# Up-projection of split activations with one 512-column matmul per k-tile, its two bank halves added on evacuation

## The reference

```python
def conv_geglu_ffn(x, w_up, conv_w, conv_b, w_down):      # once; D_FF = 5504
    up = einsum('bsd,df->bsf', x, w_up)                   # 2048 -> 2 * 5504
    u = pad(up, 2 rows in front)
    u = sum(u[:, j:j + S] * conv_w[j] for j in range(3)) + conv_b
    gate, val = split(u, 2, axis=-1)
    y = gelu(gate, approximate=True) * val
    return einsum('bsf,fd->bsd', y, w_down)

def second_ffn(x, w1, w2):                                # twice; 2048 -> 8192 -> 2048
    return square(relu(x @ w1)) @ w2
```

## Time and profile before

| what | value |
|---|---|
| median of 3 runs | 3329.59 us (3329.06 to 3329.69) |
| span of the profiled execution, first to last instruction | 3327.3 us |
| mean granted TensorE clock | 0.986 |
| first up stage, 86 units | about 467 to 964 us |
| second up stage, 64 units | about 1540 to 1910 us |
| third up stage, 64 units | about 2593 to 2963 us |

### The profile page before, as it was taken

The page is one execution under the profiler, slowest core; times in us unless marked ns, Lnnn a source line. Parts: engine busy times, 40 slices in busy tenths (PEclk is TensorE's granted clock), DMA queues, the critical chain, the costliest instruction groups (busy, mean ns, idle before and its releaser), DMA issues.

```text
span 3327.3 us, 54721 instructions
## 1 busy us (share of the span) xinstructions
PE 3210.2 (96%) x21428; PEld 2969.3 (89%) x21428; DVE 1948.1 (59%) x2303; ACT 1510.5 (45%) x1684; POOL 11.0 (0%) x25
## 2 busy tenths in 40 slices
PE   7999989999999979998999999998999899999998
PEld 7999779999998879878999988888988899998886
DVE  6666566566554469866444444448985644444445
ACT  5565554444444444654333444444654433344443
POOL 0000000000000000000000000000000000000000
PEclk9999999999999989999999999999999999999999
DMA  6444435554555544344455555554435455555553
GB/s 223 153 158 157 175 145 186 177 188 176 185 220 197 192 141 159 146 146 157 178 188 177 183 220 189 194 197 150 143 125 194 152 178 187 177 215 189 192 197 127
DMA packets 81366, 585.27 MB, mean 176 GB/s; under 512 B 9072, under 2 KB 9072, under 8 KB 11392
## 3 DMA queue, kind: packets, MB, share of 16 engines
q1 hardware_dynamic: 78912, 567.78, 47.6%
q0 software_dynamic: 2368, 16.35, 1.3%
HBM read 581.99 MB, written 2.10 MB: 176 GB/s over the span
## 4 chain that ended last, share of the span: by engine, by line
PE 90%; DVE 4%; issue 2%; ACT 2%; DMA 1%; DVEq 0%; SPq 0%; ACTq 0%
PE bank L536 35%; PE bank L524 17%; PE bank L526 17%; PE bank L525 17%; DVE store L1485 1%; DVE w_lo L1192 1%; ACT w_hi L847 1%; PE bank L567 1%; DMA raw<-units 1%; PE bank L573 0%; PE bank L693 0%; PE bank L692 0%; PE bank L691 0%; ACT L962 0%; PE bank L723 0%
## 5 line engine op out<-in xcount | busy, mean ns | idle before, releaser
L1192 DVE TENSOR_TENSOR w_lo<-raw,w_hi 128x2048 fp32r<-128x2048 f32 x543 | 1230.9, 2268 | 870.7 <-ACT y_hi L851 575.3
L524 PE MATMUL bank<-x_hi,w_hi 128*128 128x256 f32 x4928 | 1402.7, 285 | 8.1 <-DVE x_lo L1213 5.6
L525 PE MATMUL bank<-x_lo,w_hi 128*128 128x256 f32 x4928 | 1395.7, 283 | 0.0
L526 PE MATMUL bank<-x_hi,w_lo 128*128 128x256 f32 x4928 | 1395.7, 283 | 0.0
L847 ACT ACTIVATE w_hi<-raw 128x2048 fp32r<-128x2048 f32 x543 | 1028.6, 1895 | 703.5 <-PE bank L536 644.4
L524 PEld LDWEIGHTS bank<-x_hi,w_hi 128*128 128x128 f32 x4928 | 947.0, 192 | 12.3 <-DVE w_lo L1192 6.9
L525 PEld LDWEIGHTS bank<-x_lo,w_hi 128*128 128x128 f32 x4928 | 947.3, 192 | 0.2
L526 PEld LDWEIGHTS bank<-x_hi,w_lo 128*128 128x128 f32 x4928 | 947.0, 192 | 0.0
L536 PE MATMUL bank<-w_hi,y_hi 128*128 128x512 f32 x1752 | 470.2, 390 | 11.3 <-DVE y_lo L1195 6.1
L536 PE MATMUL bank<-w_lo,y_hi 128*128 128x512 f32 x1752 | 469.9, 390 | 0.0
L536 PE MATMUL bank<-w_hi,y_lo 128*128 128x512 f32 x1752 | 469.9, 390 | 0.0
(11 more groups left out here) (209 smaller groups left out, 1398.5 us busy)
## 6 DMA issues: line engine op xcount, KB each, us to landing
raw<-units SPq DMA_DIRECT2D x527, 1024.0 KB, 4.8
gain_b<-rows POOLq DMA_DIRECT2D x7, 1024.0 KB, 7.4
bias_b<-rows POOLq DMA_DIRECT2D x6, 1024.0 KB, 9.7
raw<-units SPq DMA_DIRECT2D x8, 768.0 KB, 4.2
raw<-units SPq DMA_DIRECT2D x8, 512.0 KB, 3.7
x<-x_in SPq DMA_DIRECT2D x2, 1024.0 KB, 8.4
out<-x SPq DMA_DIRECT2D x2, 1024.0 KB, 3.9
store<-attn_consts POOLq DMA_DIRECT2D x1, 1024.0 KB, 14.8
```

The lines of the kernel that those rows point to most:

```text
L524: pe.matmul(acc, hi, x_hi[:, k, :], start=(k == 0), stop=False)
L525: pe.matmul(acc, hi, x_lo[:, k, :], start=False, stop=False)
L526: mm = pe.matmul(acc, lo, x_hi[:, k, :], start=False, stop=(k == KT - 1))
L1192: ins = dve.tensor_tensor(w_lo[:, slot, 0:width], raw[:, slot, 0:width], w_hi[:, slot, 0:width].bitcast(F32), ALU.subtract)
```

## The change

In the up stages `x_hi` and `x_lo` lie side by side for each k-tile in one tensor `x_hl`. For each k-tile one matmul of 512 columns moves both past w_hi: x_hi goes to the first half of the bank, x_lo to the second. A second matmul of 256 columns adds w_lo with x_hi to the first half. From the second k-tile on the narrow matmul is issued ahead of the wide one. The two halves of the bank have to be added: ScalarE copies the second half out (`up_low_half`), VectorE adds the first half to it (`up_sum`), and the bank is free after that (`up_added`). In the first block the middle tap, its scale and bias move to VectorE as a tensor_scalar on `up_sum`, and the other taps read `up_sum` in place of the bank. In the second block ReLU and square become one instruction on VectorE. The two new tiles lie in the space of `lat_lo`. The other stages read `x_hi` and `x_lo` as views of the new tensor.

```diff
-        x_hi = sb("x_hi", [P, KT, S], F32R)
-        x_lo = sb("x_lo", [P, KT, S], F32R)
+        x_hl = sb("x_hl", [P, KT, 2, S], F32R)
+        x_hi, x_lo = x_hl[:, :, 0, :], x_hl[:, :, 1, :]
...
+        up_low_half, up_sum = (sb(n, [P, S], offset=at[0] - 4 * S * (QT + VT - i)) for i, n in enumerate(
+            ("up_low_half", "up_sum")))
...
+            def wide_unit(stage, turn, s, layer, acc, x_event=None):
+
+                pe.wait_ge(lo_done, unit_of(stage, turn, s, layer) + 1)
+                slot = stage.slot(s)
+
+                def high(k):
+                    return pe.matmul(acc[:, :], w_hi[:, slot, k * P:(k + 1) * P], x_hl[:, k, :, :],
+                                     start=(k == 0), stop=(k == KT - 1))
+
+                def low(k):
+                    return pe.matmul(acc[:, 0:S], w_lo[:, slot, k * P:(k + 1) * P], x_hi[:, k, :],
+                                     start=False, stop=False)
+
+                for k in range(KT):
+                    if x_event is not None and k % 2 == 0:
+                        pe.wait_ge(xt_lo, x_event * 8 + (k // 2 + 1))
+                    if k == 0:
+                        high(k)
+                    low(k)
+                    if k:
+                        mm = high(k)
+                mm.then_inc(unit_mm, 1)
...
             def up1(turn, s):
                 if not first_turn(turn):
-                    pe.wait_ge(conv_done, turn * 3 + (s - 2))
-                column_unit(UP1, turn, s, 0, bank[s][:, 0:S], x_event=1 if first_turn(turn) and s == 0 else None)
+                    pe.wait_ge(up_added, turn * 3 + (s - 2))
+                wide_unit(UP1, turn, s, 0, bank[s], x_event=1 if first_turn(turn) and s == 0 else None)
...
-                    act.activation(x_hi[:, 2 * b:2 * b + 2, :].rearrange("p a c -> p (a c)"), bank[b][:, :],
+                    act.activation(x_hi[:, 2 * b:2 * b + 2, :], bank[b][:, :].rearrange("p (a c) -> p a c", a=2),
                                    ACT.Copy).then_inc(xt_hi, 1)
...
-                    act.activation((ffn_gate, ffn_val)[n][:], bank[s][:, 0:S], ACT.Identity,
-                                   scale=column(cols1, first + 2, pair * 8), bias=column(cols1, first + 3, pair * 8)
-                                   ).then_inc(conv_base, 1)
+                    if not (first_turn(turn) and s == 0):
+                        act.wait_ge(up_added, pair * 2 + n)
+                    act.activation(up_low_half[:], bank[s][:, S:2 * S], ACT.Copy).then_inc(up_low, 1)
...
-                    act.activation(ffn_gate[:], bank[s][:, 0:S], ACT.Relu).then_inc(relu_read, 1)
+                    act.wait_ge(up_added, layer * FT2 + 2 * FT1 + i)
+                    act.activation(up_low_half[:], bank[s][:, S:2 * S], ACT.Copy).then_inc(up_low, 1)
...
-                    dve.wait_ge(conv_base, pair * 2 + (n + 1))
-                    chain = Chain(dve, conv_step, pair * 2 + n, 1)
-                    chain.link(dve.scalar_tensor_tensor(to[:, 1:S], acc[:, 0:S - 1], column(cols1, first + 1, pair * 8),
+                    dve.wait_ge(up_low, pair * 2 + (n + 1))
+                    chain = Chain(dve, conv_step, pair * 2 + n, 2)
+                    if not (first_turn(pair) and n == 0):
+                        dve.wait_ge(conv_done, pair * 2 + n)
+                    dve.tensor_tensor(up_sum[:], bank[s][:, 0:S], up_low_half[:], ALU.add).then_inc(up_added, 1)
+                    dve.wait_ge(up_added, pair * 2 + (n + 1))
+                    chain.link(dve.tensor_scalar(to[:], up_sum[:], column(cols1, first + 2, pair * 8),
+                                                 column(cols1, first + 3, pair * 8), ALU.mult, ALU.add))
+                    chain.link(dve.scalar_tensor_tensor(to[:, 1:S], up_sum[:, 0:S - 1], column(cols1, first + 1, pair * 8),
                                                         to[:, 1:S], ALU.mult, ALU.add))
-                    dve.scalar_tensor_tensor(to[:, 2:S], acc[:, 0:S - 2], column(cols1, first, pair * 8),
+                    dve.scalar_tensor_tensor(to[:, 2:S], up_sum[:, 0:S - 2], column(cols1, first, pair * 8),
                                              to[:, 2:S], ALU.mult, ALU.add).then_inc(conv_done, 1)
...
-                    dve.wait_ge(relu_read, layer * FT2 + i + 1)
-                    dve.tensor_tensor(slot_at(i), ffn_gate[:], ffn_gate[:], ALU.mult).then_inc(y2_ready, 1)
+                    dve.wait_ge(up_low, layer * FT2 + 2 * FT1 + i + 1)
+                    if not (first_turn(turn) and s == 0):
+                        dve.wait_ge(y2_ready, layer * FT2 + i)
+                    dve.tensor_tensor(up_sum[:], bank[s][:, 0:S], up_low_half[:], ALU.add).then_inc(up_added, 1)
+                    dve.wait_ge(up_added, layer * FT2 + 2 * FT1 + i + 1)
+                    dve.scalar_tensor_tensor(slot_at(i), up_sum[:], 0.0, up_sum[:], ALU.max, ALU.mult).then_inc(y2_ready, 1)
```

More of the change, by code:

```diff
@@ L379, in build @@
             "qd_step", "kd_step", "d_maxstep", "d_normstep", "d_rsstep", "d_mixstep"))
-        conv_base, conv_done, conv_step, gelu_done, y_ready = (sem(n) for n in (
-            "conv_base", "conv_done", "conv_step", "gelu_done", "y_ready"))
+        up_low, up_added = sem("up_low"), sem("up_added")
+        conv_done, conv_step, gelu_done, y_ready = (sem(n) for n in ("conv_done", "conv_step", "gelu_done", "y_ready"))
         (pad_zero, gate_ready, h_ready, dw_step, c_copied, c_ms, c_rs, c_rsstep, c_step, cn_ready, c_hi, c_lo,
@@ L402, in build @@
         diag_ready, last_conv, last_copied = sem("diag_ready"), sem("last_conv"), sem("last_copied")
-        relu_read, y2_ready = sem("relu_read"), sem("y2_ready")
+        y2_ready = sem("y2_ready")
         stored = sem("stored")
@@ L674, in _ @@
                 row_begin(DOWN1, s, 0, 1)
-            pe.wait_ge(conv_done, 2 * FT1)
+            pe.wait_ge(up_added, 2 * FT1)
             row_stage(DOWN1, 0, 1)
@@ L821, in up2 @@
                     if not first_turn(turn):
-                        pe.wait_ge(relu_read, layer * FT2 + turn * 3 + (s - 2))
-                    column_unit(UP2, turn, s, layer, bank[s][:, 0:S],
-                                x_event=layer * 2 + 3 if first_turn(turn) and s == 0 else None)
+                        pe.wait_ge(up_added, layer * FT2 + (2 * FT1 - 2) + turn * 3 + s)
+                    wide_unit(UP2, turn, s, layer, bank[s],
+                              x_event=layer * 2 + 3 if first_turn(turn) and s == 0 else None)
                 for s in range(SLOTS):
@@ L830, in _ @@
                     row_begin(DOWN2, s, layer, 1)
-                pe.wait_ge(relu_read, (layer + 1) * FT2)
+                pe.wait_ge(up_added, (layer + 1) * FT2 + 2 * FT1)
                 row_stage(DOWN2, layer, 1)
@@ L1020, in up1_pair @@
                     act.wait_ge(unit_mm, unit_of(UP1, turn, s, 0) + 1)
[L1021 to L1026, removed]
-                    act.activation((ffn_gate, ffn_val)[n][:], bank[s][:, 0:S], ACT.Identity,
-                                   scale=column(cols1, first + 2, pair * 8), bias=column(cols1, first + 3, pair * 8)
-                                   ).then_inc(conv_base, 1)
+                    if not (first_turn(turn) and s == 0):
+                        act.wait_ge(up_added, pair * 2 + n)
+                    act.activation(up_low_half[:], bank[s][:, S:2 * S], ACT.Copy).then_inc(up_low, 1)
                 act.wait_ge(conv_done, pair * 2 + 1)
+                if not first_turn(pair):
+                    act.wait_ge(y_ready, pair)
                 act.activation(ffn_act[:], ffn_gate[:], ACT.Gelu_apprx_tanh).then_inc(gelu_done, 1)
@@ L1170, in up2 @@
                     act.wait_ge(unit_mm, unit_of(UP2, turn, s, layer) + 1)
-                    if not (first_turn(turn) and s == 0):
-                        act.wait_ge(y2_ready, layer * FT2 + i)
-                    act.activation(ffn_gate[:], bank[s][:, 0:S], ACT.Relu).then_inc(relu_read, 1)
+                    act.wait_ge(up_added, layer * FT2 + 2 * FT1 + i)
+                    act.activation(up_low_half[:], bank[s][:, S:2 * S], ACT.Copy).then_inc(up_low, 1)
                 for s in range(SLOTS):
@@ L1212, in transposed @@
                     at_ = (slice(None), slice(2 * b, 2 * b + 2), slice(None))
-                    dve.tensor_tensor(x_lo[at_].rearrange("p a c -> p (a c)"), bank[b][:, :],
-                                      x_hi[at_].rearrange("p a c -> p (a c)").bitcast(F32), ALU.subtract).then_inc(xt_lo, 1)
+                    dve.tensor_tensor(x_lo[at_], bank[b][:, :].rearrange("p (a c) -> p a c", a=2),
+                                      x_hi[at_].bitcast(F32), ALU.subtract).then_inc(xt_lo, 1)
             def sharpened(eps, chain, *roots):
@@ L1406, in up1_pair @@
                     first = COLS1["conv"][0] + 4 * n
-                    acc, to = bank[s], (ffn_gate, ffn_val)[n]
-                    dve.wait_ge(conv_base, pair * 2 + (n + 1))
-                    chain = Chain(dve, conv_step, pair * 2 + n, 1)
```

(6 more changed lines are left out.)

## The result

The changed kernel takes 3305.36 us (median of 4 runs, 3303.59 to 3306.39), the kernel before 3329.64 us (3329.06 to 3329.93). The ratio is 0.9928, with a 95% interval of 0.9916 to 0.9940. The gain is 24.3 us where 45.0 us were forecast, and the time lies 7 us above the upper end of the range.

The account below looks back on a forecast made before the run. TensorE was taken as the bound, busy 96% of the span. Saving 45.7 us over 214 units, less 0.6 us for first units, all else free, gave -45.0 us: 3329.6 to 3284.6 us, range 3279 to 3298.

Parts of the forecast that it names:

- Point 1: TensorE, up stages' steady state: a k-tile falls from 360.0 to 346.7 ns, 213 ns a unit, 45.7 us over 214 units.
- The surplus goes by matmul, not by column: TensorE steps: each matmul, of 256 or 512 columns, carries 13.3 ns beyond its column time, saved with each matmul removed.
- The prediction's own last sign of being wrong: Profile after, up stages: the forecast is wrong if the wide matmul's step is longer than 0.227 us.
- VectorE did not bind: Rival, 6%: VectorE becomes the bound in the first up stage; 18.3 us of gain lost, 3302.9 us.
- The surplus did not belong to w_hi and w_lo: Rival, 4%: the surplus comes from changing between w_hi and w_lo, the removed step nearly free; time stays 3329.6 us.
- A narrow step was at times 6.7 ns shorter: Rival, 4%: a narrow matmul behind a wide one has no surplus; k-tile 333.3 ns, gain 90 us, 3239.6 us.
- No load stood in the open: Rival, 2%: the wide matmul's load can't run beside the narrow one before it; 327 us slower, 3657 us.
- Point 2: First unit of each of three up stages gains nothing, since unit 1 waits for w_lo; 0.6 us taken off.
- Points 3, 4, 6: ScalarE's copies, second-block VectorE work (3.2 us plus links in 5.55 us), banks freed about 1 us after: all cost nothing.
- Point 7: Transfers, SP and POOL: none added; 1 MB a unit in 5.55 us, 189 GB/s, under the down stage's 197 GB/s.
- Point 5: VectorE, first block, the tight place: a pair takes 10.0 us of TensorE's 11.09 us, fitting with 1.1 us to spare.
- Point 8: Interleaved x_hi and x_lo, transposes' evacuations writing two runs of 256: taken as nothing, bound 2.9 us.

Follow-up runs that it names:

- e9: Changed kernel with each unit's narrow matmuls in one group, each moving 128 columns instead of 256, same load of 128 weights: 3270.83 us.
- e11: Changed kernel with each unit's narrow matmuls in one group, each moving 128 columns and loading 64 weight columns: 3109.34 us.
- e1: Changed kernel with an up unit's order altered to 15 wide matmuls, the 16 narrow ones, then the last wide one: 3290.69 us, ratio 0.9883 to the kernel before.
- e7: Changed kernel in its own order, narrow matmuls taking w_hi for weights instead of w_lo: 3304.38 us.
- e3: Changed kernel with its new evacuation, but each wide matmul made as two of 256 columns: 3329.30 us, ratio 1.0001 to the kernel before.
- e5: Changed kernel in its own order, narrow matmuls writing the second half of the bank instead of the first: 3306.33 us.
- e10: Changed kernel with each unit's narrow matmuls in one group, each loading 64 weight columns instead of 128, 256 columns moved: 3271.66 us.
- e13: Changed kernel in its own alternating order, each narrow matmul with 64 weight columns instead of 128: 3278.15 us.
- e8: Changed kernel with an up unit's order altered to one wide, four narrow, four wide, four narrow and so on: 3299.63 us.
- e15: Changed kernel with each unit's narrow matmuls in one group and 64 weight columns in all up-stage matmuls: 3273.12 us.
- e4: Changed kernel with the narrow matmuls of the up stages left out, 16 wide ones a unit: 2974.68 us.

## Why the prediction was wrong

**Point 1, steady state: wrong, and by all of the miss.** The step that failed is "after it costs one wide and one narrow matmul: 226.7 + 120.0 = 346.7 ns". The term came out as 352.9 ns: 113 ns saved a unit, not 213. "The surplus goes by matmul, not by column" was read from two uniform streams, each of which gives one number; that they agree at 13.3 ns looked like a law. It is none for narrow matmuls: their steps are 120.0, 113.3, 112 or 59.9 ns by what they load and move (e9 to e11). That the order makes the loss is shown by e1; by what mechanism a narrow matmul and its neighbour's load lengthen each other is not. The prediction's own last sign of being wrong is the one that came: a wide step longer than 0.227 us.

**The evidence for the mixed stream was read too short.** The earlier trace rows was quoted for its first step, 0.12 us from narrow to wide. The surplus comes behind that: the group of four wide matmuls in that row lasts 1.09 us, that of the earlier trace rows 1.07. The steps of the kernel before at this place are 234, 235, 229, 232, 231 and 227 ns, 27.7 ns over the steady ones, the transient that e1 shows. It was in the trace before.

**The range.** Both bounds of the mixed k-tile, 320 and 360 ns, were named, and the range then left the upper one to a rival of 4%. What lies between 346.7 and 360 ns, where the result fell, had no case of its own. A composition never seen in the trace should have kept more of the width between its bounds.

**The rivals.** None happened. VectorE did not bind, TensorE never waiting for it inside a stage. The surplus did not belong to w_hi and w_lo (e7). A narrow step was at times 6.7 ns shorter (113 ns), but the wide ones took more back. No load stood in the open: the extra is 6 ns a k-tile, not 110. The rule of the Trainium skill's page "TensorE: Matmul & The Clock Gate", section "Wait — 56ns, not 53.3ns?" would have given 8.6 us as an estimate; by the runs a removed matmul was worth 113 / 16 = 7.1 ns, between its 2.5 and my 13.3.

**Point 2** held: in the second up stage unit 1 starts 7.1 us behind the first x_lo, before and after. **Points 3, 4, 6** held together, by e3. **Point 7** held: TensorE is never without work in the two stretches above, at 188 and 185 GB/s. In point 4 the ReLU and square (L1625) took 0.425 us, not 0.48. **Point 5** held and was near: a pair in the first block, VectorE of the changed kernel,

```profile
525.29 0.42 DVE L1432 TENSOR_TENSOR up_sum<-bank,up_low_half 128x256 f32<-128x256 f32 x1 [1.07 <-ACT up_low_half L1048]
525.91 0.41 DVE L1434 TENSOR_SCALAR ffn_val<-up_sum,cols 128x256 f32<-128x256 f32 x1 [0.19 <-DVE up_sum L1432]
526.47 0.49 DVE L1436 SCALAR_TENSOR_TENSOR ffn_val<-up_sum,cols,ffn_val 128x255 f32<-128x255 f32 x1
527.10 0.48 DVE L1438 SCALAR_TENSOR_TENSOR ffn_val<-up_sum,cols,ffn_val 128x254 f32<-128x254 f32 x1
527.79 0.43 DVE L1442 TENSOR_TENSOR store<-ffn_act,ffn_val 128x256 f32 x1 [0.21 <-DVE ffn_val L1438]
528.14 2.28 DVE L1212 TENSOR_TENSOR w_lo<-raw,w_hi 128x2048 fp32r<-128x2048 f32 x1
...
530.95 0.43 DVE L1432 TENSOR_TENSOR up_sum<-bank,up_low_half 128x256 f32<-128x256 f32 x1 [0.53 <-ACT up_low_half L1048]
```

waits 1.07 and 0.53 us for ScalarE's copies, 1.6 us of a pair of 11.3; forecast were 1.1 of 11.09. The links cost 0.15 to 0.27 us, where each was put at 0.15. **Point 8** held: eight x_lo operations take 4.88 us (4.87 before).

## What stays open

Why a run of wide matmuls begins with five long steps behind narrow ones, and four to ten behind a pause, is not settled. In alternation neither the bank's half, nor the k-tile moved, nor the weights' tensor matters (e5 to e7); the five long steps don't go with the narrow matmul's load (e10). No run tells the size of the load from the number of partitions written. And like units can differ: e13's by turns, e8's from stage to stage. The extras in the table are, within a nanosecond, multiples of 6.67 ns, 16 periods at 2.4 GHz, which hints at something counted, and no more than that was shown.

## What to carry to other kernels

A step time taken from a uniform stream of matmuls holds for that stream; where a change mixes widths, look for a junction in the trace and read ten steps behind it, not one. With loads of 128 weights, matmuls of 256 and 512 columns in turn lost about half of the expected gain here: order the matmuls of a unit in one group of each kind instead, which gave 3290.69 us in place of 3305.36 (and lost 40 ns a unit where all loads were halved, e15). A kernel with the new evacuation and the old matmuls (e3) cleared several points of the sum at once.

## What the runs showed of the hardware that was not expected

- The step of a 256-column matmul at 2.4 GHz among its like: 120.0 ns with a load of 128 weight columns, 113.3 ns with 64 (e10); with 128 columns, 112 (e9) and 59.9 ns (e11). The step of a 512-column one: 226.7 ns with 128, 230.0 ns, unsteady, with 64 (e15). With 64, half the partitions are written too.
- A wide and a narrow matmul in turn take 352.9 ns with full loads and 340.8 ns with halved ones.
- Behind a run of narrow matmuls (e1) or a pause (e4), wide steps are too long, by up to 13 ns, for four to ten steps; behind a pause the very first is 335 to 341 ns.
- With halved narrow loads in alternation, like units take 5.477 and 5.557 us by turns (e13).
- The order of the same 32 matmuls moves a unit from 5.567 to 5.647 us.
